# Two projections of a hybrid decoder block: pairs of column groups in eight banks, and two of eight steps by seven block products

## The reference, cut to what matters

```python
proj = rmsnorm(h, norm_w) @ w_in            # 18432 columns: q, k, v, gates of both branches
o_ret  = rmsnorm(retention(rq, rk, rv)) * silu(rz)
o_diff = rmsnorm(diff_attention(dq, dk, dv, lam), subln_w) * 0.8 * silu(dz)
mixed = sigmoid(g_ret) * (o_ret @ w_ret_up) + sigmoid(g_diff) * (o_diff @ w_diff_up)
h = h + mixed @ w_out
return rmsnorm(h, final_norm_w)
```

## Time and profile before

| | us |
|---|---|
| median of 3 runs | 1092.07 (1091.98 to 1092.58) |
| the profiled execution, its span | 1090.7 |
| PE busy in the span | 1080.9 |
| DVE busy | 686.6 |
| ACT busy | 528.6 |
| POOL busy | 47.1 |

### The profile page before, as it was taken

How to read it: one execution, slowest core, us unless ns; L and a number is a source line. 1 busy time by engine, 2 the same in 40 slices (tenths; PEclk the granted TensorE clock), 3 DMA queues, 4 the chain that set the end, 5 groups by cost and what they waited for, 6 DMA issues and landing times.

```text
span 1090.7 us, 13141 instructions
## 1 busy us (share of the span) xinstructions
PE 1080.9 (99%) x4888; PEld 899.3 (82%) x4888; DVE 686.6 (63%) x848; ACT 528.6 (48%) x689; POOL 47.1 (4%) x63
## 2 busy tenths in 40 slices
PE   9999999999999999999999999999999999999997
PEld 7888888888888888888888888888888888888885
DVE  6685575485566455567766767576757676676554
ACT  6554455344455433344654464446544554444443
POOL 0100000000000000000100002000200020000111
PEclk9999999999999999999999999999999999999999
DMA  9877667666667555667576766766677666666862
GB/s 324 304 247 219 182 196 209 193 195 212 193 175 226 192 194 193 193 179 242 170 216 185 220 199 197 211 202 196 205 209 212 195 206 203 211 207 210 320 214 102
DMA packets 141072, 227.97 MB, mean 209 GB/s; under 512 B 14416, under 2 KB 40784, under 8 KB 140240
## 3 DMA queue, kind: packets, MB, share of 16 engines
q1 hardware_dynamic: 140448, 223.98, 66.6%
q10 hardware_dynamic: 560, 3.15, 0.7%
HBM read 210.84 MB, written 2.10 MB: 195 GB/s over the span
## 4 chain that ended last, share of the span: by engine, by line
PE 98%; issue 1%; DMA 1%; SPq 0%; DVE 0%; ACT 0%; ACTq 0%; POOLq 0%; POOL 0%; DVEq 0%
PE bank L1228 31%; PE bank L1226 31%; PE bank L1227 31%; PE bank L1236 1%; PE bank L1235 1%; PE bank L1234 1%; DMA raw<-w_in_dram 1%; PE bank L1313 0%; PE bank L1198 0%; PE bank L1250 0%; PE bank L1249 0%; PE bank L1248 0%; PE bank L1205 0%; PE bank L1202 0%; PE bank L1270 0%
## 5 line engine op out<-in xcount | busy, mean ns | idle before, releaser
L806 DVE TENSOR_TENSOR w_lo<-raw,w_hi 128x1024 fp32r<-128x1024 f32 x380 | 471.1, 1245 | 370.8 <-ACT w_hi L562 369.9
L562 ACT ACTIVATE w_hi<-raw 128x1024 fp32r<-128x1024 f32 x380 | 403.0, 1061 | 520.5 <-PE bank L1228 489.4
L1226 PE MATMUL bank<-w_hi,xt_hi 128*128 128x512 f32 x1264 | 493.1, 390 | 0.0
L1228 PE MATMUL bank<-w_hi,xt_lo 128*128 128x512 f32 x1264 | 491.9, 389 | 0.0
L1227 PE MATMUL bank<-w_lo,xt_hi 128*128 128x512 f32 x1264 | 491.8, 389 | 0.0
L1228 PEld LDWEIGHTS bank<-w_hi,xt_lo 128*128 128x128 f32 x1264 | 237.2, 188 | 49.4
L1227 PEld LDWEIGHTS bank<-w_lo,xt_hi 128*128 128x128 f32 x1264 | 237.3, 188 | 48.8
L1226 PEld LDWEIGHTS bank<-w_hi,xt_hi 128*128 128x128 f32 x1264 | 237.3, 188 | 48.7
L1226 PE MATMUL bank<-w_hi,ot_hi 128*128 128x512 f32 x256 | 99.6, 389 | 0.0
L1227 PE MATMUL bank<-w_lo,ot_hi 128*128 128x512 f32 x256 | 99.6, 389 | 0.0
L1228 PE MATMUL bank<-w_hi,ot_lo 128*128 128x512 f32 x256 | 99.6, 389 | 0.0
(11 more groups left out here) (112 smaller groups left out, 473.4 us busy)
## 6 DMA issues: line engine op xcount, KB each, us to landing
raw<-w_in_dram SPq DMA_DIRECT2D x284, 512.0 KB, 4.2
raw<-w_ret_up_dram SPq DMA_DIRECT2D x32, 512.0 KB, 4.1
raw<-w_diff_up_dram SPq DMA_DIRECT2D x32, 512.0 KB, 4.3
raw<-w_out_dram SPq DMA_DIRECT2D x32, 512.0 KB, 4.4
rot<-squares_t SPq DMA_DIRECT2D x96, 64.0 KB, 2.4
zs<-squares_t SPq DMA_DIRECT2D x48, 64.0 KB, 2.2
normed<-squares_t SPq DMA_DIRECT2D x48, 64.0 KB, 2.2
raw<-w_in_dram SPq DMA_DIRECT2D x8, 256.0 KB, 5.9
```

The costliest lines, as they stand in the source:

```text
L562: act.activation(w_hi[:, s, :, :], raw[:, s, :, :], ACT.Copy).then_inc(hi_ready, 1)
L806: dve.tensor_tensor(w_lo[:, s, :, :], raw[:, s, :, :], w_hi[:, s, :, :].bitcast(F32), ALU.subtract) \
L1226: pe.matmul(bank[bk][:, :], hi, w_hi[:, s, kk, :], start=k == 0, stop=False)
L1228: return pe.matmul(bank[bk][:, :], lo, w_hi[:, s, kk, :], start=False, stop=k == KT - 1)
```

## The change

For `w_ret_up` and `w_out` two column groups are taken together: a unit is now one feature tile by 1024 columns, still 512 KB and 12 matmuls, and a pair of groups has 16 units (k = 0 to 15) and fills four "own" banks. There are two pairs in each of the two projections; the other stages keep their units. Of the eight pairs of feature tiles, those at k = 4, 5 and k = 10, 11 (`SEVEN_AT`) are computed as a 2x2 block product by seven block products (Strassen's scheme in Winograd's form) instead of eight: 7 x 3 = 21 matmuls in place of 24. Four of the seven go by sums that must be formed: sums of token tiles once for each projection (`sum_tokens`, L974 to L986 and L991), and four sums of weight blocks for each such step (`sum_weights`, L950 to L956; `round_sums`; `rest_of_sums`, L970). Part of the seven is gathered in the four other banks ("shared"), which are joined once for each pair of groups (`copy_first`, `join_shared`, L999 to L1004) and then added (`merge_ret` L1227, or `add_shared` L1353 and `add_own` L1361).

A step of seven waits for both units of its pair: `sum_weights` stands in DVE's order ahead of the split of the unit before, `round_seven` waits for `units_done` of one unit later than an ordinary rounding, and both units are released together after nine matmuls (`seven_by_weights`); twelve more (`seven_by_sums`) come after the next unit. PE's last two units of each pair of groups are computed bank by bank (`pair_last`).

```diff
+PAIR_COLS = 2 * COLS
+PAIRED = (U_UP, U_OUT)
+PAIR_GROUPS = D // PAIR_COLS
+SEVEN_AT = (2, 5)
+N_SEVEN = len(SEVEN_AT)
+SUMS = 4
...
+def pair_banks(group):
+    own, shared = (4, 5, 6, 7), (0, 1, 2, 3)
+    return (own, shared) if group % 2 == 0 else (shared, own)
+def pair_blocks(group):
+    p = group % PAIR_GROUPS
+    return ((0, 2 * p + 1), (0, 2 * p), (1, 2 * p + 1), (1, 2 * p))
...
+                elif paired(n)[0] is not None:
+                    group, k = paired(n)
+                    first = (group % PAIR_GROUPS) * PAIR_COLS
+                    sp.dma_start(raw[:, s, :, :], w[:, k, first:first + PAIR_COLS].rearrange("p (a c) -> p a c", a=KU)) \
...
+            for e in range(SUMS):
+                weigh(e)
             for b in range(BLOCKS):
-                pool.wait_ge(h_norm_step, 4 * b + 5)
+                weigh(SUMS + 2 * b)
+                pool.wait_ge(h_row_step[b], 4)
...
+            def round_seven(n, group, u):
+                s = n % RING
+                act.wait_ge(units_done, n + 2)
+                for i in range(2):
+                    act.wait_ge(raw_landed[s + i], (n - s) * 4 + 16)
+                act.activation(hi_blocks[:, KU * s + 1:KU * s + 4, :], raw_blocks[:, KU * s + 1:KU * s + 4, :], ACT.Copy) \
+                   .then_inc(hi_ready, 2)
...
+            def round_sums(group, u):
+                count = sevens_before(group, u)
+                act.wait_ge(weight_sums_ready, count + 1)
+                if count:
+                    act.wait_ge(sevens_done, count)
+                act.activation(v_hi[:, :, :], weight_sums(group)[:, :, :], ACT.Copy).then_inc(sum_hi_ready, 1)
...
+                if group is not None and k % KU == 0 and k // KU - 1 in SEVEN_AT:
+                    round_sums(group, k // KU - 1)
...
+            square_h(SUMS)
+            square_h(SUMS + 1)
+            square_h(SUMS + 2)
+            scale_h(0)
+            square_h(SUMS + 3)
+            scale_h(1)
...
+            def sum_weights(n, group, u):
+                s, count = n % RING, sevens_before(group, u)
+                for i in range(2):
+                    dve.wait_ge(raw_landed[s + i], (n - s) * 4 + 16)
+                b12, b22, b21 = KU * s, KU * s + 2, KU * s + 3
+                dve.tensor_tensor(weight_sums(group)[:, 0, :].rearrange("p (a n) -> p a n", a=2), raw_blocks[:, b12 + 1:b12 + 3, :],
+                                  raw_blocks[:, b12:b12 + 1, :].broadcast_to([P, 2, COLS]), ALU.subtract) \
+                   .then_inc(weight_sums_step, 1)
+                dve.wait_ge(weight_sums_step, 2 * count + 1)
+                dve.tensor_tensor(weight_sum(group, 2), raw_blocks[:, b22, :], weight_sum(group, 0), ALU.add).then_inc(weight_sums_step, 1)
+                dve.wait_ge(weight_sums_step, 2 * count + 2)
+                dve.tensor_tensor(weight_sum(group, 3), raw_blocks[:, b21, :], weight_sum(group, 2), ALU.subtract) \
+                   .then_inc(weight_sums_ready, 1)
...
+                s = n % RING
+                dve.wait_ge(hi_ready, n + 2)
+                three = slice(KU * s + 1, KU * s + 4)
+                dve.tensor_tensor(lo_blocks[:, three, :], raw_blocks[:, three, :], hi_blocks[:, three, :].bitcast(F32),
+                                  ALU.subtract).then_inc(units_split, 4)
...
+            def join_shared(group):
+                b1, b5, b6, b7 = pair_banks(group)[1]
+                parts = [shared_part(group, i) for i in range(SUMS)]
+                dve.wait_ge(sevens_done, N_SEVEN * (group + 1))
+                dve.wait_ge(first_copied, group + 1)
+                dve.tensor_tensor(parts[1], parts[0], bank[b6][:, :], ALU.add).then_inc(shared_step, 1)
+                dve.wait_ge(shared_step, 2 * group + 1)
+                dve.tensor_tensor(parts[2], parts[1], bank[b7][:, :], ALU.add).then_inc(shared_step, 1)
+                dve.wait_ge(shared_step, 2 * group + 2)
+                dve.tensor_tensor(parts[3], parts[2], bank[b5][:, :], ALU.add)
+                dve.tensor_tensor(parts[1], parts[1], bank[b5][:, :], ALU.add).then_inc(shared_drained, 1)
...
+                group, k = paired(n)
+                ahead, k_ahead = paired(n + 1)
+                if ahead is not None and k_ahead % KU == 0 and k_ahead // KU in SEVEN_AT:
+                    sum_weights(n + 1, ahead, k_ahead // KU)
+                if group is not None and k // KU in SEVEN_AT:
+                    if k % KU == 0:
+                        rest_of_seven(n, group, k // KU)
+                    return
                 dve.wait_ge(hi_ready, n + 1)
                 dve.tensor_tensor(w_lo[:, s, :, :], raw[:, s, :, :], w_hi[:, s, :, :].bitcast(F32), ALU.subtract) \
                    .then_inc(units_split, 2)
+                if group is not None and k % KU == 0 and k // KU - 1 in SEVEN_AT:
+                    rest_of_sums(group, k // KU - 1)
...
+            def merge_ret(group, i):
+                b, j = pair_blocks(group)[i]
+                part = shared_part(group, i)
+                own_full(group, i)
+                dve.tensor_tensor(part, part, bank[pair_banks(group)[0][i]][:, :], ALU.add).then_inc(own_drained, 1)
+                dve.wait_ge(own_drained, SUMS * group + i + 1)
+                cols = slice(j * COLS, (j + 1) * COLS)
+                dve.tensor_tensor(mixed[:, b, cols], mixed[:, b, cols], part, ALU.mult)
+            for s in range(FIRST, FIRST + PAIR_GROUPS * KT):
+                split_lo(U_UP + (s + AHEAD), (s + AHEAD) % UNITS)
+                if s % KT == KT - AHEAD:
+                    join_shared(s // KT)
+                if s % KT in (KT - 1, 0):
+                    for i in range(2):
+                        merge_ret((s - 1) // KT, 2 * (s % KT == 0) + i)
...
+            def add_shared(group):
+                for i in range(SUMS):
+                    b, j = pair_blocks(group)[i]
+                    part = gate[:, b, j * COLS:(j + 1) * COLS]
+                    dve.tensor_tensor(part, part, shared_part(group, i), ALU.add).then_inc(pair_joined, 1)
...
+                if g == GROUPS_D - 1 and u == 5:
+                    dve.wait_ge(mt_lo_ready, SEVEN_AT[-1] + 1)
+                    sum_tokens(1, xt_hi, xt_lo)
+                if g == GROUPS_D - 1 and u == 7:
+                    rest_of_token_sums(1)
+                out_s = s - GROUPS_D * UNITS
+                if out_s > 0 and out_s % KT == KT - AHEAD:
+                    group = PAIR_GROUPS + out_s // KT
+                    join_shared(group)
                     dve.wait_ge(x_again, 32)
...
+                    dve.wait_ge(shared_drained, group + 1)
+                    add_shared(group)
+                if out_s in (KT - 1, KT):
+                    for i in range(2):
+                        add_own(PAIR_GROUPS, 2 * (out_s - (KT - 1)) + i)
...
+            add_own(group, 0)
+            add_own(group, 1)
+            square_half(0, j)
+            add_own(group, 2)
+            mean_square(0, j, SUMS)
+            add_own(group, 3)
+            square_half(1, j)
+            mean_square(1, j, SUMS + 2)
+            scale_h(0, j)
+            scale_h(1, j)
...
+            def pair_last(n, k, own, t_hi, t_lo):
+                pe.wait_ge(units_split, 2 * (n + 1) + (2 * RING + 2))
+                for i in range(SUMS):
+                    for kk in range(KU):
+                        mm = pair_product(n + kk, k + kk, i, own, t_hi, t_lo)
+                    if i < SUMS - 1:
+                        mm.then_inc(own_filled, 1)
+                mm.then_inc(units_done, KU)
...
+            def seven_by_weights(n, k, own, shared, t_hi, t_lo):
+                u = k // KU
+                a, first, last = SEVEN_AT.index(u), u == SEVEN_AT[0], u == SEVEN_AT[-1]
+                b11, b22, b21 = (KU * (n % RING) + i for i in (1, 2, 3))
+                pe.wait_ge(units_split, 2 * (n + 1) + (2 * RING + 2))
+                by_weight(own[0], tile_of(t_hi, k + 1, 0), tile_of(t_lo, k + 1, 0), hi_blocks[:, b21, :], lo_blocks[:, b21, :],
+                          False, False)
+                by_weight(own[1], xsum_hi[:, a, 3, :], xsum_lo[:, a, 3, :], hi_blocks[:, b22, :], lo_blocks[:, b22, :],
+                          False, False)
+                by_weight(shared[0], tile_of(t_hi, k, 0), tile_of(t_lo, k, 0), hi_blocks[:, b11, :], lo_blocks[:, b11, :],
+                          first, last).then_inc(units_done, KU)
...
+            def seven_by_sums(group, k, own, shared, t_hi, t_lo):
+                u = k // KU
+                a, first, last = SEVEN_AT.index(u), u == SEVEN_AT[0], u == SEVEN_AT[-1]
+                pe.wait_ge(sum_lo_ready, sevens_before(group, u) + 1)
+                by_weight(own[2], tile_of(t_hi, k + 1, 1), tile_of(t_lo, k + 1, 1), wsum_hi[:, 3, :], wsum_lo[:, 3, :], False, False)
+                for bk, x_sum_at, w_sum_at in ((shared[1], 0, 0), (shared[2], 1, 2), (shared[3], 2, 1)):
```

(22 more changed lines are left out.)

306 lines of the change are left out of this document (204 added, 102 removed).

## The result

The changed kernel takes 1106.47 us in the median of 4 runs (1104.58 to 1109.03), the kernel before 1092.11 (1091.98 to 1092.58): a ratio of 1.0132, 95% interval 1.0118 to 1.0147. It is slower, as forecast, but by 14.4 us where 7.7 were forecast, and outside the range, whose upper end was 1104.5. The profiled execution is the longest of the four: 1109.03, with a span of 1106.8, against 1090.7 before. In all four runs the time is 2.2 us above the span, where the prediction added 1.4.

A forecast was written before the change was run, and what follows sets the result against it. PE was taken to bound the kernel (98% of the chain). 1090.7 - 5.4 + 3.5 + 5.9 + 0.2 + 3.6 gave a span of 1098.5, and with 1.4 above the span 1099.8 us; range 1096 to 1104.5.

The forecast's parts named there:

- 24 matmuls: On PE, 21 matmuls for 24 at two steps in each of four pairs of groups: 5.4 us less.
- `w_ret_up`, second pair: PE waits for DVE's merges and weight sums: unit 19 late by 1.6 us, unit 20 by 1.9, sum 3.5.
- `w_out`, units 3 to 8: Start of `w_out`: PE waits for splits behind token sums, weight sums, `merge_diff` and small DMAs; 2.7 us in all.
- `w_out`, unit 9: Its split stands behind weight sums that wait for the load of unit 11; PE 3.2 us late.
- clock behind it: Rival: PE's clock falls in the longest stall, with the later load 1103 to 1106 us; chance 0.17 (1102 to 1106).
- `w_out`, second pair: Costed like `w_ret_up`'s second pair, with two plain adds in place of two merges: 0.2 us.
- tail: After the last matmul, late joins and additions on DVE put the last scaling 3.6 us later than before.
- a meeting of load 11 with its beginning: In `w_out`, if unit 11's load met the start of `x`, the stall ahead of unit 9 would be 5.0 us.
- Unit 12: In `w_out`, its load under the reading of `x` has 7.8 us to land and was taken as in time.
- the faster rival: DVE's queue quicker than added up, no stall at units 16 to 20 or `w_out` 0 to 11: 1088.2 us; chance 0.07.
- its low end: Low end of the whole forecast's range: -5.4 + 3.1 + 3.4 + 3.0, 4.1 us above before, 1096.

The follow-up runs named there:

- `fill_stall`: Changed kernel plus twenty useless matmuls with zeros on PE ahead of unit 9 of `w_out`, filling its idle time; median 1103.95 us.
- `weigh_late`: Changed kernel with POOL's four products in `w_out`'s second pair held until its first step's seven products are done; median 1107.29 us.
- `best3`: Changed kernel with seven products, weight sums, small DMAs and POOL's products moved, `x` loaded in four pieces, tail reordered; 1088.12 us, 0.9966 of the kernel before.

## Why the prediction was wrong

The direction and most of the places came as forecast, but the size did not: the clock and the meeting of unit 9's load with `x`, which the sum left out, and POOL beside DVE, which it did not know, make the difference. Term by term, in the profiled execution:

| term | forecast | measured |
|---|---|---|
| 24 matmuls | -5.4 | -5.4 |
| `w_ret_up`, second pair | 3.5 | 2.6 |
| `w_out`, units 3 to 8 | 2.7 | 1.1 |
| `w_out`, unit 9 | 3.2 | 6.1 |
| clock behind it | a rival | 2.8 |
| `w_out`, second pair | 0.2 | 2.9 |
| tail | 3.6 | 4.2 |
| first 75 us | 0 | 1.3 |

The sum of the measured is 15.6 of 16.1; the rest lies in delays of 0.1 us and less that the table leaves out. The distance of the time from the span, 2.2 us where I had 1.4, adds 0.8 that the table does not have.

**Unit 9** (2.9 too little). The step that failed is the time at which `x` is asked for. I put it behind the split of unit 8, at 22.5 us after PE's unit 0, and wrote that a meeting of load 11 with its beginning would cost 5.0. Even by my own times `x` came before that load had landed (25.2), and the sum gave the overlap nothing. It came at 18.9. Both sides of that difference came 1.8 us sooner than I had them (PE could start at 28.0 for 29.8, and wanted to at 24.8 for 26.6), so that the difference is right and its two terms are not; that the shifts are equal is in part luck. Unit 12 was luck too. Its load had 7.8 us by the prediction and took 9.0, and only the stall ahead of unit 9 gave it that time.

**The clock** (2.8, priced at 0 in the forecast). I read the earlier trace rows as: 3.5 us of idle PE do not lower it. In the runs here it fell behind gaps of 2.5, 3.2, 3.7, 3.8, 4.0 and 6.1 us, and not behind gaps of 1.6 and 2.0. So even my own 3.2 would have lowered it, and the forecast, had all else held, should have been near 1102.5. The rival was right and had 0.17; by `fill_stall` it is shown that the idle time of PE brings the clock down.

**Second pair of `w_out`** (2.7 too little). I costed it by analogy with `w_ret_up`, by two adds for two merges, and gave DVE's instructions the durations of a DVE that works alone. POOL's products were in the earlier trace rows; that they work beside the weight sums was to be seen in the order, and what that does to DVE I had no row for. `weigh_late` shows it.

**Units 19 and 20 of `w_ret_up`, units 3 to 8 of `w_out`** (2.5 too much). A dependent DVE instruction starts 0.03 us after the end of the one that it waits for (418.02 after 416.77 + 1.22), and I had taken 0.18 from the earlier trace rows, where a custom instruction follows an addition. Weight sums cost 2.6 for 2.97, a pair of merges 2.6 for 3.0 and the token sums 2.7 for 3.6, so that the load of unit 5 was also issued 0.9 us sooner. Here the errors ran the other way and hid a part of the others.

**The tail** (0.6 too little). The last scaling is 2.9 us later, where I had 3.6. But I measured only to the scaling: the four stores, which lay apart before, now leave together, and the last lands 1.3 us later.

The profiled execution is also 2.6 above its own median. About half of that stands in its first 12 us, where its matmuls start 0.43 us apart up to 9.8 us, the distance of the lower clock, though the row of that stretch gives 1.00; why is not shown; the rest I can't place, since only this run has a trace. That DVE would be quick enough (the faster rival, 1088.2) was wrong for this order of work; `best3`, at 1088.1, shows that it is right for another. That the two numbers are so near is luck: the rival counted a tail 1.6 us longer, and `best3` has 0.9. One slip in the range: its low end took 3.0 for the tail whose own low end stood at 1.6; with that it would have been 1094.8.

## What to carry over

A saving on the busiest engine is worth its length only if what feeds it is on time at every unit; add up the feeder's queue with what stands beside it, a second engine that uses the same memory, and with the loads that it waits for. An instruction that waits for a load does not belong ahead of one that is due: put it behind, or bring the load forward. A large transfer that competes for the DMA engines is best cut into pieces and spread over stages that have room, and a stall as long as those behind which the clock fell here (2.5 us and more) should be costed with the slow matmuls behind it.

## What I had not expected of the hardware

- While POOL multiplies tiles of 512, DVE's instructions on SBUF take 0.6 to 1.1 us longer: 2.33 for 1.22, 1.67 for 0.69, 2.29 for 1.22. POOL's product takes 1.3 at its shortest, and up to 2.8 in these stretches. The lengths add up as if the two took turns, which no run tests by itself: in `weigh_late` DVE's instruction of 1065.99 kept its 1.29, and the product that started at 1066.15 took 2.28.
- Eight DMAs of 64 KB took 2.2 us each to land alone and 9.7 beside a 2 MB load on another queue.
- A DMA on ACT's queue was issued at 1015.90, while two activations that stand before it in the program started at 1016.24 and 1016.76.
- A dependent DVE instruction follows 0.03 us after the end of the one it needs.
- A gap of 2.5 us on PE brought the granted clock to the lower level, two gaps of 0.85 and 1.56 us with 2.6 us of matmuls between them did not.
